# Expert-table copies issued from GpSimd instead of ScalarE, with a bound on how many are under way

## The reference, cut to what matters

```python
        mod = cs @ w_ada[l] + b_ada[l]          # modulation: shifts, scales, gates
...
        u = expert_u[idx]
        v = expert_v[idx]
        act = jax.nn.gelu(jnp.einsum('td,thkd->thk', xt, u))
        return jnp.einsum('thk,thkd->td', (g * act).astype(xt.dtype), v)
```

## Time and profile before

| | us |
|---|---|
| median of 3 runs | 1623.56 (1617.5 to 1631.35) |
| the profiled execution, its time | 1618.68 |
| its span, first to last instruction | 1616.8 |
| TensorE busy | 1437.2 (89%) |
| VectorE busy | 1099.1 (68%) |
| ScalarE busy | 785.9 (49%) |
| GpSimd busy | 271.7 (17%) |

### The profile page before, as it was taken

The page is one execution under the profiler, slowest core; times in us unless marked ns, Lnnn a source line. Parts: engine busy times, 40 slices in busy tenths (PEclk is TensorE's granted clock), DMA queues, the critical chain, the costliest instruction groups (busy, mean ns, idle before and its releaser), DMA issues.

```text
span 1616.8 us, 24506 instructions
## 1 busy us (share of the span) xinstructions
PE 1437.2 (89%) x8308; PEld 1077.5 (67%) x8308; DVE 1099.1 (68%) x2390; ACT 785.9 (49%) x1804; POOL 271.7 (17%) x317
## 2 busy tenths in 40 slices
PE   9998999999899999998499889999977887777887
PEld 8887999998789999997499885444422232222222
DVE  6756877676568676576378668766666667666654
ACT  6646544356466344464385444444444454444433
POOL 1000010000000000000000013433333333333331
PEclk9999999999999999989699999999999999999999
DMA  9998799978996999869999859999999999999996
GB/s 322 340 366 316 267 378 385 386 286 282 359 362 226 375 385 347 277 228 335 323 348 360 312 191 380 422 421 421 421 422 421 422 420 421 422 421 421 420 422 271
DMA packets 119268, 578.23 MB, mean 358 GB/s; under 512 B 11472, under 2 KB 11616, under 8 KB 85904
## 3 DMA queue, kind: packets, MB, share of 16 engines
q0 software_dynamic: 44768, 297.78, 44.9%
q10 hardware_dynamic: 35248, 136.42, 24.7%
q1 hardware_dynamic: 39168, 142.97, 24.1%
HBM read 576.08 MB, written 135.27 MB: 440 GB/s over the span
## 4 chain that ended last, share of the span: by engine, by line
PE 48%; DMA 26%; DVE 9%; ACT 8%; issue 5%; ACTq 3%; SPq 0%; DVEq 0%; POOL 0%; POOLq 0%
DMA attn<-expert_uv,idx 12%; DMA ring<-wstream 9%; PE PS L1144 8%; PE PS L1108 7%; PE PS L620 5%; PE PS L616 5%; PE PS L611 5%; DMA late<-expert_uv,idx 5%; ACTq L1199 3%; PE PS L744 3%; PE PS L1071 2%; PE PS L642 2%; ACT wrg L1581 2%; DVE early_splits L1656 2%; PE PS L854 2%
## 5 line engine op out<-in xcount | busy, mean ns | idle before, releaser
L1656 DVE TENSOR_TENSOR early_splits<-ring,early_splits 128x1024 fp32r<-128x1024 f32 x166 | 202.2, 1221 | 76.8 <-ACT early_splits L1223 76.3
L2350 DVE CUSTOM_DVE_ANT_0 late<-late,PS 128x1024 f32<-128x1024 f32 x128 | 156.2, 1220 | 112.8 <-DMA late<-expert_uv,idx 112.8
L2350 DVE CUSTOM_DVE_ANT_0 attn<-attn,PS 128x1024 f32<-128x1024 f32 x128 | 156.1, 1220 | 97.0 <-DMA attn<-expert_uv,idx 95.6
L1223 ACT ACTIVATE early_splits<-ring 128x1024 fp32r<-128x1024 f32 x166 | 174.9, 1055 | 74.6 <-DMA ring<-wstream 43.4
L1144 PE MATMUL PS<-late,wrg 128*128 128x512 f32 x288 | 145.4, 630 | 43.4 <-ACT wrg L1581 43.4
L1573 ACT ACTIVATE gel<-dot 128x1 f32<-128x1 f32 x256 | 51.2, 200 | 266.8 <-DVE dot L2350 266.6
L1144 PE MATMUL PS<-attn,wrg 128*128 128x512 f32 x288 | 142.3, 619 | 31.7 <-ACT wrg L1581 31.2
L558 POOL DMA_INDIRECT attn<-expert_uv,idx x128 | 121.3, 948 | 248.1 <-PE PS L1144 103.1
L558 POOL DMA_INDIRECT late<-expert_uv,idx x128 | 119.9, 936 | 231.9 <-PE PS L1144 116.9
L1144 PEld LDWEIGHTS PS<-late,wrg 128*128 128x128 f32 x288 | 49.9, 191 | 135.5 <-ACT wrg L1581 98.1
L1144 PEld LDWEIGHTS PS<-attn,wrg 128*128 128x128 f32 x288 | 50.7, 193 | 123.3 <-ACT wrg L1581 80.9
(11 more groups left out here) (412 smaller groups left out, 3008.9 us busy)
## 6 DMA issues: line engine op xcount, KB each, us to landing
ring<-wstream SPq DMA_DIRECT2D x258, 512.0 KB, 9.8
expert_uv<-expert_u ACTq DMA_DIRECT2D x64, 1024.0 KB, 20.0
expert_uv<-expert_v ACTq DMA_DIRECT2D x64, 1024.0 KB, 20.8
ada<-w_ada POOLq DMA_DIRECT2D x32, 512.0 KB, 9.6
late<-w_ada POOLq DMA_DIRECT2D x16, 512.0 KB, 8.9
late<-wstream SPq DMA_DIRECT2D x4, 512.0 KB, 11.1
attn<-expert_uv,idx POOLq DMA_INDIRECT x128, 15.2
late<-expert_uv,idx POOLq DMA_INDIRECT x128
```

What stands on the lines that cost most here:

```text
L1223: act.activation(hi_of(u), raw(u), ACT.Copy).then_inc(hi_ready, 1)
L1656: ve.tensor_tensor(lo_of(u), raw(u), hi_of(u).bitcast(F32), ALU.subtract).then_inc(units_begun, 1)
L2350: ve.tensor_tensor_reduce(row, row, H2N[n // 8], 1.0, 0.0, ALU.mult, ALU.add, dot[:, n % 2, k:k + 1]).then_inc(dot_ready, 1)
```

## The change

GpSimd issues all 128 copies; ScalarE issues none. GpSimd's new order is: the first three modulation loads; 26 copies; nine modulation turns (first feed-forward), with one copy behind the first and one behind the second load of each turn; 30 copies; six modulation turns in the same form; 12 copies; the wait for the end of the second feed-forward and the four weight loads; 30 copies; `subk`; the gathers. In the runs of 26, 30, 12 and 30 copies, each waits until the third one before it has landed, so at most three are under way; the 30 copies beside the turns wait for nothing but the turn's own `ada_used`. The first gather waits for all of them, by four semaphores in place of one. Bytes, sizes and the table are the same.

```diff
+UNDER_WAY = 3
...
-        tables_joined = sem("tables_joined")
+        rows_joined, joined_beside = [sem(f"rows_joined{k}") for k in range(UNDER_WAY)], sem("joined_beside")
...
+            joined, paced = [0], [0]
+
+            def join_rows(count):
+
+                for c in range(joined[0], joined[0] + count):
+                    table, half = ((expert_u, slice(0, D)), (expert_v, slice(D, 2 * D)))[c % 2]
+                    rows = slice(c // 2 * JOIN_ROWS, (c // 2 + 1) * JOIN_ROWS)
+                    k, nth = paced[0] % UNDER_WAY, paced[0] // UNDER_WAY
+                    if nth:
+                        gp.wait_ge(rows_joined[k], 16 * nth)
+                    gp.dma_start(expert_uv[rows, half], table[rows, :]).then_inc(rows_joined[k], 16)
+                    paced[0] += 1
+                joined[0] += count
+
+            def ada_and_rows(first, end):
+
+                at = joined[0]
+                with gp.Fori(first, end) as i:
+                    for s in range(ADA_SLOTS):
+                        gp.wait_ge(ada_used, i * ADA_SLOTS + (s + 1 - ADA_SLOTS))
+                        gp.dma_start(ada_parts[s],
+                                     w_ada[bass.ds(i * ADA_SLOTS + s, 1)].rearrange("o p e -> (o p) e")
+                                     ).then_inc(ada_landed[s], 16)
+                        if s < 2:
+                            table, half = ((expert_u, slice(0, D)), (expert_v, slice(D, 2 * D)))[s]
+                            rows = bass.ds(i * JOIN_ROWS + (at // 2 - first) * JOIN_ROWS, JOIN_ROWS)
+                            gp.dma_start(expert_uv[rows, half], table[rows, :]).then_inc(joined_beside, 16)
+                joined[0] += 2 * (end - first)
+
             for s in range(ADA_SLOTS):
                 gp.dma_start(ada_parts[s], w_ada[s]).then_inc(ada_landed[s], 16)
-            with gp.Fori(1, 48 // ADA_SLOTS) as i:
-                for s in range(ADA_SLOTS):
-                    gp.wait_ge(ada_used, i * ADA_SLOTS + (s + 1 - ADA_SLOTS))
-                    gp.dma_start(ada_parts[s],
-                                 w_ada[bass.ds(i * ADA_SLOTS + s, 1)].rearrange("o p e -> (o p) e")).then_inc(ada_landed[s], 16)
+            turns = 1 + ADA_FF0 // ADA_SLOTS
+            join_rows(26)
+            ada_and_rows(1, turns)
+            join_rows(30)
+            ada_and_rows(turns, 48 // ADA_SLOTS)
+            join_rows(12)
...
                 gp.dma_start(dst, src).then_inc(latent_loaded, 16)
 
+            join_rows(30)
+            assert joined[0] == JOINS
             gp.wait_ge(split_begun, WA_AT)
...
-                    gp.wait_ge(tables_joined, 16 * JOINS)
+                    gp.wait_ge(joined_beside, 16 * (JOINS - paced[0]))
+                    for j in range(UNDER_WAY):
+                        gp.wait_ge(rows_joined[j], 16 * (paced[0] // UNDER_WAY + (j < paced[0] % UNDER_WAY)))
...
-                act.dma_start(expert_uv[rows, half], table[rows, :]).then_inc(tables_joined, 16)
...
-                    join_rows()
-                    if s % 5 == 0:
-                        join_rows()
...
-                    if c < HELD - 1:
-                        join_rows()
...
-                        join_rows(i=i, m=m)
...
-                join_rows()
...
-                join_rows()
-                join_rows()
...
-                join_rows()
```

More of the change, by code:

```diff
@@ L1186, in _ @@
             act.wait_ge(blank_set, 1)
-            joined = [0]
-            def join_rows(i=None, m=0):
-                c = joined[0] if i is None else m
-                table, half = ((expert_u, slice(0, D)), (expert_v, slice(D, 2 * D)))[c % 2]
-                if i is None:
-                    rows = slice(c // 2 * JOIN_ROWS, (c // 2 + 1) * JOIN_ROWS)
-                    joined[0] += 1
-                else:
-                    rows = bass.ds(i * JOIN_ROWS + joined[0] // 2 * JOIN_ROWS, JOIN_ROWS)
-                act.dma_start(expert_uv[rows, half], table[rows, :]).then_inc(tables_joined, 16)
             def squares(src, chunks=KC, updated=None, dst=SQ):
@@ L1393, in feed_forward @@
                         split_hi(u + 3 * m + 1, i)
-                        join_rows(i=i, m=m)
                         split_hi(u + 3 * m + 2, i)
-                joined[0] += NF - 4
                 u += 3 * (NF - 4)
@@ L1538, in _ @@
             act.activation(RECH[:, KC - 1, :], XC[:, KC - 1, :], ACT.Copy).then_inc(rech_ready, 1)
-            assert joined[0] == JOINS
             for j in range(4):
```

## The result

The changed kernel takes 1542.76 us (median of 4 runs, 1541.6 to 1544.2) beside 1621.7 us for the kernel before (1617.5 to 1631.35). The ratio is 0.952, with a 95% interval of 0.9486 to 0.9555: 4.8% faster. The profiled executions have spans of 1541.5 and 1616.8 us, 75.3 us apart. The forecast was 45 us; the sign was right and the size was not.

A forecast was written before the change was run, and what follows sets the result against it. It took ScalarE standing in copy issues its full queue refused, idling TensorE 57 us outside the feed-forwards. Terms 24 + 8 + 9 + 1 + 5 = 47, less 2, gave 45 us: 1623.56 - 45 = 1578.6, said as 1578, range 1556 to 1612.

The forecast's parts named there:

- 47 us of idle time outside the feed-forwards: Attention, second network: gains of 24 (gate and lru), 8 and 9 (attention), 1 and 5 us (830 to 900, 900 to 955).
- -2 us in the feed-forwards: Feed-forward turns: a loss between 0 and 0.6 us a turn over 15 turns, 9 us at most, taken as 2 us.
- The mechanism outside the feed-forwards: Attention and second network: ScalarE stands inside copy issues its full queue does not take, 10.47 us against 0.53 free.
- The clock term: Gate and lru stage: half-speed work at a granted clock of 0.83 lifts the most from 25.2 to about 31 us.
- The discounts on idle time: Outside the feed-forwards: of 57 us idle, 47 taken: 24 of 25.2, 8 and 9 of 10.8 each, 1 of 2.5, 5 of 7.7.
- Both limits touch: Feed-forward turn of 17.91 us: DMA at 381 GB/s and TensorE's 17.6 us of matmuls both bound it.
- The landing of the third modulation part: Feed-forward turns: queued behind two copies, it lands after about 12 to 14 us in place of 9.5.
- Margin over 60 us: Second network: the last 30 copies are done by 837 to 844 us, the first gather comes at some 910 us.
- The bytes rule: Whole kernel: DMA engines were full, so only free issues come off, 18 us, giving 1606 us; chance 0.13.
- The slower rival: Feed-forward turns: modulation queued behind copies makes a turn 22.5 us, 69 us over 15 turns, giving 1647 us; chance 0.08.
- More than that: Whole kernel: the clock and softmax chain give back all idle time, 57 + 6 us, giving 1561 us; chance 0.12.
- The issue price on GpSimd: GpSimd's queue: 1 us per copy issue, from a load's 0.53 and a gather's 0.98 us; 128 us in all.

The follow-up runs named there:

- free_issues: Changed kernel plus 128 issues on ScalarE at the copies' old places, each a 16-row copy into an unread table; real copies stay on GpSimd: 1549.73 us, ratio 0.9586.
- second_40_scalar: Changed kernel with the second network's 40 copies back on ScalarE at their old places, GpSimd issuing the other 88: 1591.81 us, ratio 0.9791.
- old_counts_gpsimd: Changed kernel with the earlier counts on GpSimd, 26, 6 and 40 copies in place of 30, 12 and 30: 1558.89 us, ratio 0.9606.
- turns_behind_12: Changed kernel with each turn's two copies behind its second and third modulation part in place of first and second: 1542.69 us, ratio 0.9495.
- turns_from_scalar: Changed kernel with the 36 copies of the feed-forward turns issued by ScalarE where they stood before, the other 92 as changed: 1564.1 us, ratio 0.9681.
- under_way_2: Changed kernel with two copies under way in place of three: 1554.53 us, ratio 0.9615.
- small_copies_gpsimd: Changed kernel with copies cut to 16 of 256 rows and gathers reading another tensor, so the experts' values are left out: 1542.24 us, ratio 0.9545.
- second_32_scalar: Changed kernel with 32 second-network copies back on ScalarE, one beside each gate product, and 34 in GpSimd's run of layer 1: 1574.75 us, ratio 0.967.
- under_way_1: Changed kernel with one copy under way in place of three: 1717.88 us, ratio 1.0626.
- under_way_8: Changed kernel with eight copies under way in place of three: 1541.24 us, ratio 0.9538.

## Why the prediction was wrong

**Where the 30 us are.** The forecast was 47 us of idle time outside the feed-forwards, nothing for the clock and -2 us in the feed-forwards. By the windows TensorE's idle time outside the feed-forwards fell by 47.7 us: 8.6 and 8.4 in the attention stages, 25.2, -0.1 and 5.6 in the second network. The busy time fell by 22.1 us, and the idle time in the two feed-forwards by 5.6 us. Together that is the 75.3 us. So the term that was worked out came out right, and two were missing: the clock, and the gain in the feed-forwards.

**Right.** The mechanism outside the feed-forwards: with the issues on GpSimd the long issues end, no wait of several us stands ahead of the takes (the one wait of ScalarE for "issue" is 2.4 us), and the stages follow. Two pairs show it. free_issues: 128 issues that find room cost 7 us. second_40_scalar and old_counts_gpsimd have the same counts in the same stages and differ in the issuer of 40 copies, and with it in their pacing: 1591.8 and 1558.9 us, 33 us, of which 40 free issues can be 2 or 3 (by free_issues). One reading of the rows was off: the 2.68 us of the earlier trace rows are not inside the issue of 10.47 us, which ends at 765.50 us, but are the next issue. The take waited 11.36 us for both:

```profile
765.54 2.68 ACTq L1199 DMA_DIRECT2D expert_uv<-expert_v  x1
768.26 0.38 ACT L1234 ACTIVATE late<-PS 128x256 f32<-128x256 f32 x1 [11.36 <-issue]
```

**The clock term was mis-sized.** The forecast put the half-speed work of the gate and lru stage at 6 us (25.2 to 31) and then took none of it. By the windows, from 698 to 955 us (now 665.5 to 880.3) TensorE lost 30.7 us of idle time and 11.6 us of busy time; over the kernel the busy time fell by 22.1 us. The clock was low for more than the idle gaps: in the kernel before, the records show the lower level (1.2 GHz) for 20.5 us in a row from 787 us, over a gap of 10.6 us and the lru products on both sides of it. The step that failed is that the term was kept to one stage and then dropped: in the gate and lru stage it was 7.9 us, in the attention of layer 1, with a granted clock of 0.97, 5.2 us, and 22.1 us in all.

**The discounts on idle time were right as a sum, and in part by luck.** I took 47 of 57 us outside the feed-forwards. After the change 9 us idle there are left of 57 (2.2, 2.4, 0, 2.5 and 2.1 in the five windows), so 47.7 us went. The attention stages' 8 and 9 us met 8.6 and 8.4. In the gate and lru stage all 25.2 us went and not 24, at 830 to 900 us none of the 1 us, and 5.6 in place of 5 behind it. No run parts these terms from one another, so the reasons given for each discount are not shown.

**The feed-forwards had the wrong sign: -2 forecast, +9.8 measured.** By the windows it is 9.4 us, 5.6 of them idle time. The step that failed is "Both limits touch", with 381 GB/s and 17.6 us of TensorE for a turn of 17.91 us. Neither was a limit: in the changed kernel's turns the rate is 397 GB/s (190 to 320 us; 384 before, 200 to 330 us), and its turns take 17.3 us in feed-forward 0 and 17.0 in feed-forward 1 (17.7 and 17.6 before; the 17.91 us were the mean of four turns of feed-forward 1). Nor is this gain the stall's: in the kernel before no issue in a feed-forward was long. Those of feed-forward 0 took 0.58 us at most, and line 1199 from 505 to 698 us, feed-forward 1, reads:

```profile
L1199 ACTq DMA_DIRECT2D expert_uv<-expert_u x9: 540/540/571, 514.8 to 658.4; - x9
L1199 ACTq DMA_DIRECT2D expert_uv<-expert_v x9: 529/529/552, 523.0 to 666.9; - x9
```

The forecast had noted that two queues give the ring a half and not a third, and used it only to make a loss smaller. The landing of the third modulation part was put at 12 to 14 us, but its terms (11 less 7, 2.7 and 2) add up to 8.7; it was 14.9 us, and no gain was lost by it that the runs show (turns_behind_12). turns_from_scalar brings back the 2.3 us of feed-forward 0, with the ring at 14.0 us. It cannot part the third queue from the two issues per turn there, as free_issues, with nearly two queues, the ring at 9.5 us and the issues, also takes 150.4 us. In the end of feed-forward 1 they part: free_issues 68.5 us, turns_from_scalar 81.4.

**A margin was named and was not one.** "Margin over 60 us" for the last 30 copies was measured to the first gather. The work between that they meet is the query's side loads, from about 812 us. The copies end about there, which the forecast did not look at, so that was luck; ten more cost 16 us (old_counts_gpsimd), and a slower pace 9 us there (under_way_2). Part of this is in the 42 us of the second network: old_counts_gpsimd gets 26.2 of them by the other issuer alone, the counts give the other 16.

**The rivals.** The bytes rule (1606 us) is refuted by the gate and lru stage, whose share stayed at 1.0 while its time fell from 90 to 57 us, and by small_copies_gpsimd, where without the bytes the time fell no further. A busy share of 1 was no sign of a bound. The Trainium skill, "DMA: Bandwidth & Descriptors", section "Issuing engines are not separate DMA queues", says that another issuer saves only the sequencer's time and that this is usually small. free_issues agrees for issues that find room (7 us for 128); where they find none it does not hold here (33 us for 40 copies, second_40_scalar against old_counts_gpsimd, the pacing with it). The slower rival did not come from the copies in the turn; second_32_scalar and under_way_1 show where it does. "More than that" (1561 us) had the direction and not the reason: it gave back all 57 us of idle time, of which 9 stayed, and left out the feed-forwards and most of the clock. The issue price on GpSimd, 1 us by bounds of 0.53 and 0.98, was 0.55 us.

**Open.** What made the turns of feed-forward 0 take 150 us, the third queue or the issues. Whether a bound of its own on ScalarE would have done as well as the move to GpSimd: with at most three copies outstanding none of its issues was long in the kernel before, so it may, but no kernel with such a bound was run, and the waits for it would stand on ScalarE too.

## What to carry to other kernels

A DMA issue that is cheap when few transfers are outstanding (0.52 us here) can hold its engine when many are (up to 11.4 us on ScalarE, mostly with six or seven 1 MB copies out), and everything behind it waits. So put bulk copies on the queue of an engine that has nothing else to do then, with the order written out so that each stretch of copies ends before that engine must bring something else. Look for the deadline at every transfer that the copies can meet, not at their reader alone; and when TensorE idles in gaps, count the low clock of the work behind them as well as the gaps.

## What the runs showed of the hardware

- Queue depth of the copies did not matter to the other queue: with 3 and with 8 copies of 1 MB under way on GpSimd the ring's 512 KB loads landed after 9.1 us, while the copies took about 15 and 35 us.
- ScalarE stood in issues of 1 MB copies (over 1 us, up to 11.4) in 25 of 30 with six or seven of its copies outstanding, and in none of 55 with at most three; GpSimd stood in none of 71 with seven outstanding (under_way_8).
- With three queues busy each got a third of the packets (122, 120 and 121 in 4 us, turns_from_scalar), with two a half (393 and 388 in 7 us, the kernel before).
- A 1 MB copy of 4 KB rows, DRAM to DRAM, costs GpSimd 0.55 us of issue, the same as a load of half the size (0.53 us).
- TensorE's granted clock stood at its lower level for 72 us until the first gather in the kernel before, and for 10 us in the changed kernel.
